# Two 64-byte spacers in on-chip memory: where activations stand modulo 128 bytes, beside the weight rings

## The reference, cut to what matters

```python
x = x + even_mixer(rmsnorm(x, g), w_in, sink, w_out)
x = x + memory_cross_attention(rmsnorm(x, g), rmsnorm(mem, g), wq, wkv, wo)
x = x + conv_mixer(rmsnorm(x, g), w_in, conv_w, conv_b, w_out)
...
a = silu(xb @ w_gate_e[e]) * (xb @ w_up_e[e])
return a @ w_down_e[e]
```

## The kernel before

| tensor | before | modulo 128 | modulo 512 | after | modulo 128 | modulo 512 |
|---|---|---|---|---|---|---|
| `X` | 16512 | 0 | 128 | 16576 | 64 | 192 |
| `xa_hi` | 32896 | 0 | 128 | 32960 | 64 | 192 |
| `xa_lo` | 49280 | 0 | 128 | 49344 | 64 | 192 |
| `cm_hi` | 65664 | 0 | 128 | 65728 | 64 | 192 |
| `cm_lo` | 75904 | 0 | 128 | 75968 | 64 | 192 |
| `U` | 86144 | 0 | 128 | 86208 | 64 | 192 |
| `arena` | 102528 | 0 | 128 | 102592 | 64 | 192 |
| `sq` | 152704 | 0 | 128 | 152768 | 64 | 192 |
| `w_ring`, `ex_rings` | 159040 | 64 | 320 | 159168 | 64 | 448 |
| `hi_ring` | 171328 | 64 | 320 | 171456 | 64 | 448 |
| `lo_ring` | 183616 | 64 | 320 | 183744 | 64 | 448 |
| `yb_lo`, `ex_low` | 195904 | 64 | 320 | 196032 | 64 | 448 |
| `yb_hi`, `ex_raw` | 212288 | 64 | 320 | 212416 | 64 | 448 |

## Time and profile before

### The profile page before, as it was taken

How to read it: one execution, slowest core, us unless ns; L and a number is a source line. 1 busy time by engine, 2 the same in 40 slices (tenths; PEclk the granted TensorE clock), 3 DMA queues, 4 the chain that set the end, 5 groups by cost and what they waited for, 6 DMA issues and landing times.

```text
span 1635.1 us, 20099 instructions
## 1 busy us (share of the span) xinstructions
PE 1594.2 (97%) x7432; PEld 1203.1 (74%) x7432; DVE 844.8 (52%) x1456; ACT 583.8 (36%) x963; POOL 547.7 (33%) x239
## 2 busy tenths in 40 slices
PE   7999989999999999999999999999999999999997
PEld 5888768886888888887877667888877885444543
DVE  5448577125655546354668687343242544443434
ACT  4127544334332225324533342343243333112213
POOL 4441226731444444751334123455424410000000
PEclk9999999999999999999999999999999999999998
DMA  5331224521332323441222113334222349999992
GB/s 187 92 102 39 78 78 124 160 90 60 100 92 91 102 91 98 160 128 40 80 77 69 40 48 94 114 110 136 91 64 91 117 191 356 418 422 421 423 417 82
DMA packets 52787, 235.94 MB, mean 144 GB/s; under 512 B 6240, under 2 KB 7136, under 8 KB 48096
## 3 DMA queue, kind: packets, MB, share of 16 engines
q1 hardware_dynamic: 48960, 222.60, 38.8%
q0 software_dynamic: 2016, 7.34, 1.1%
q10 hardware_dynamic: 1728, 4.87, 0.9%
HBM read 230.59 MB, written 4.19 MB: 144 GB/s over the span
## 4 chain that ended last, share of the span: by engine, by line
PE 90%; DVE 6%; issue 2%; ACT 1%; DMA 0%; SPq 0%; DVEq 0%; ACTq 0%
PE G L1802 69%; PE O L1802 7%; PE S L1802 6%; PE TR L1802 4%; PE TR L1912 2%; DVE sumsq L994 1%; PE G L2374 1%; DVE sq L1054 1%; DMA w_ring<-in_stream_dram 0%; ACT hi_ring L570 0%; DVE U L1025 0%; DVE sumsq L1124 0%; DVE arena L1424 0%; DVE U L1779 0%; DVE arena L1203 0%
## 5 line engine op out<-in xcount | busy, mean ns | idle before, releaser
L535 POOL TENSOR_TENSOR lo_ring<-w_ring,hi_ring 128x1024 fp32r<-128x1024 f32 x219 | 534.0, 2440 | 788.0 <-ACT hi_ring L570 787.7
L570 ACT ACTIVATE hi_ring<-w_ring 128x1024 fp32r<-128x1024 f32 x219 | 231.3, 1059 | 587.4 <-PE G L1802 583.1
L1802 PE MATMUL G<-xa_hi,hi_ring 128*128 128x512 f32 x928 | 378.8, 408 | 9.8 <-DVE xa_lo L1116 9.7
L1802 PE MATMUL G<-xa_hi,lo_ring 128*128 128x512 f32 x928 | 364.9, 393 | 0.0
L1802 PE MATMUL G<-xa_lo,hi_ring 128*128 128x512 f32 x928 | 363.1, 391 | 0.0
L1802 PEld LDWEIGHTS G<-xa_hi,hi_ring 128*128 128x128 f32 x928 | 175.1, 189 | 48.6 <-issue 12.3
L1802 PEld LDWEIGHTS G<-xa_lo,hi_ring 128*128 128x128 f32 x928 | 175.1, 189 | 40.3 <-issue 2.6
L1802 PEld LDWEIGHTS G<-xa_hi,lo_ring 128*128 128x128 f32 x928 | 174.8, 188 | 39.8
L1802 PE MATMUL G<-yb_hi,hi_ring 128*128 128x512 f32 x388 | 154.4, 398 | 3.4 <-ACT arena L668 2.2
L1802 PE MATMUL G<-yb_hi,lo_ring 128*128 128x512 f32 x388 | 151.6, 391 | 0.0
L1802 PE MATMUL G<-yb_lo,hi_ring 128*128 128x512 f32 x388 | 151.4, 390 | 0.0
(11 more groups left out here) (350 smaller groups left out, 2501.4 us busy)
## 6 DMA issues: line engine op xcount, KB each, us to landing
w_ring<-in_stream_dram SPq DMA_DIRECT2D x219, 512.0 KB, 3.5
arena<-in_w_gu_dram SPq DMA_DIRECT2D x16, 2048.0 KB, 11.9
ex_rings<-in_w_dn_dram SPq DMA_DIRECT2D x40, 512.0 KB, 15.8
ex_low<-in_w_gu_dram SPq DMA_DIRECT2D x8, 2048.0 KB, 18.4
ex_rings<-in_w_gu_dram SPq DMA_DIRECT2D x8, 2048.0 KB, 16.0
arena<-in_w_dn_dram SPq DMA_DIRECT2D x16, 512.0 KB, 14.4
sq<-in_w_dn_dram SPq DMA_DIRECT2D x8, 512.0 KB, 18.1
X<-in_x_in_dram SPq DMA_DIRECT2D x8, 256.0 KB, 6.2
```

The costliest lines, as they stand in the source:

```text
L535: nc.gpsimd.tensor_tensor(lo_ring[:, s, :], w_ring[:, s, :], hi_ring[:, s, :], ALU.subtract).then_inc(low, 1)
L570: nc.scalar.activation(hi_ring[:, m % RING, :], w_ring[:, m % RING, :], ACT.Copy).then_inc(high, 1)
L1802: return nc.tensor.matmul(*args, **kw)
```

## The change

Two unused tensors of 16 float32 columns, 64 bytes in a partition, are declared: one ahead of `X`, one ahead of the rings. Everything from `X` to `rcp` moves up by 64 bytes, and the rings, `yb` and the `ex_` buffers by 128. No instruction is added, removed or moved, and each engine's sequence is the same; only the addresses differ.

```diff
+HALF_LINE = 16
...
+        sb("line_a", [P, HALF_LINE])
         X = sb("X", [P, KT, T])
         xa_hi = sb("xa_hi", [P, KT, T], F32R)
...
         rcp = sb("rcp", [P, 4, 2])
+        sb("line_b", [P, HALF_LINE])
         before_experts = ExitStack()
```

## The result

| | before | after |
|---|---|---|
| time, median of 6 runs | 1640.78 us (1638.08 to 1642.35) | 1626.37 us (1622.67 to 1629.88) |
| ratio | | 0.9918, 95% interval 0.9901 to 0.9935 |
| span of the profiled execution | 1635.1 us | 1626.4 us |
| mean granted clock in it | 0.991 | 0.989 |
| forecast | | 1634.1 us, range 1630.0 to 1643.5 |

The account below looks back on a forecast made before the run. PE was taken as the bound: how soon one matmul follows another. Gains of 5.6 + 2.5 + 0.3 + 0.6 less 1.0 lost make 8.0 us, so 1642.1 - 8.0 = 1634.1 us, range 1630 to 1643.5.

Parts of the forecast that it names:

- Equal places bring `yb`'s pace: 512-column fp32r matmuls on PE: equal remainders modulo 128 give 226.7 ns between starts; 8.0 us gained; chance 0.58.
- the five priced terms: Matmul pace on PE: `xa` moving 5.6, rings moving 2.5, `cm` in latents 0.3, scatter 0.6 us gained; 256 columns 1.0 lost.
- The rule behind it, modulo 128: fp32r matmuls: pace set by whether moving and stationary operands have equal remainders modulo 128; 2.2 or 6.6 ns each.
- a period of 256: Operand distances modulo 256 would be 64, 192 and after the change 0; fits all three paces, forecast of 1634.1 us holds.
- The doubt about 512: Slower rival: fp32r pace follows distance modulo 512, the change giving an untried 256; 1647 or 1655 us; chance of slower 0.15.
- `yb` itself, costed at nothing: `yb` moving against rings already has equal remainders and takes 226.7 ns; no term in the sum.
- The 256-column term: Memory tokens: 480 matmuls go from 117.9 to 120.0 ns; 1.0 us lost, bounds 0 and 1.0.
- the waits behind it, costed at nothing: PE behind the memory tokens: no term for waits; ACT, DVE and POOL groups expected as before.
- "The change doesn't touch" what lies between span and median: Whole kernel: median of runs lies 7.0 us above the profiled span, kept unchanged, so 1642.1 us was the starting point.
- the rivals: fp32r pace: only part is the remainder, 1639 or 1637.2 us (0.13); nothing changes, 1642 (0.14); slower, 1647 or 1655 (0.15).
- The page of the Trainium skill that would make the sum 0: PE operand reads: separate port for weight loads, only crossing 16-byte lines costs, so moving by 64 bytes gains 0.
- The expert stage, plain float32, DVE over `X` and `yb`, and DMAs, costed at nothing: Quads about 32.2 us, float32 matmuls 606 ns, DVE passes 683 and 689 ns, DMA at 421 GB/s; no term.

Follow-up runs that it names:

- d = 128: Kernel before plus only a 192-byte spacer ahead of the rings; `xa` start minus ring start is 128 modulo 256; 1640.73 beside 1640.26 us, ratio 1.0009.
- the first experiment: Kernel before plus two spacers of 128 bytes each, ahead of `X` and ahead of the rings; 1645.92 us, ratio 1.0038.
- the slow placements: Kernel before plus both spacers of 128 bytes (1645.92 us), or only one ahead of the rings: 192 (1640.73), 160 (1645.58), 32 bytes (1647.38).

## Why the prediction was right, and where it failed

- *Equal places bring `yb`'s pace.* Right in the traces: 226.7 ns for all 512-column pairs, -8.5 us where -8.0 was forecast. Each of the five priced terms came within 0.2 us.
- *The rule behind it, modulo 128.* It was the change's, and the prediction took it while noting that a period of 256 fits as well. The kernel with equal remainders modulo 128 and d = 128 runs at 232.3 ns: what counts is the distance modulo 256, and the change hits its one fast place because both conditions hold in it. As a test of the words "modulo 128" that was luck: a spacer of 192 bytes obeys them too and gains nothing. The doubt about 512 is settled by the spacer of 320 bytes.
- *`yb` itself, costed at nothing.* Missed, 0.7 us. Where `yb` tiles follow `xa` tiles one by one, they had up to ten slow starts each time behind the change of operand, 24 times; with equal distances the slow starts are gone.
- *The 256-column term, "1.0 us lost", and the waits behind it, costed at nothing.* This is the step that failed. The size in nanoseconds is right. But I took it for a loss on PE alone and left every wait as it was ("ACT, DVE and POOL groups as before"). The 50 ns for each unit of memory keys take away POOL's lead over DVE's addition, and two waits of 1.55 us go. So the slower part of the change brings 3.1 us where the forecast has a loss of 1.0, and some 1.3 to 2.4 us more at low clock (estimated above). The order of DVE and POOL alone, without the placement, makes the kernel 4.1 us faster. The signs stood in the trace of before: `DVE sumsq L994 1%` in the chain, and two starts 60 ns apart behind it, one of them of 2.87 us instead of 0.68.
- *"The change doesn't touch" what lies between span and median.* Wrong: executions differ in their granted clock (in the 18 runs beside the first experiment 1636.8 us goes with 0.992 and 1644.1 us with 0.987), and the change takes away waits that drops follow.
- *The range.* Its low end came from the bounds of the pace terms alone (they reach 1634.1 - 2.1 = 1632.0 us, where the prediction writes 1631.5) and a little on top. No mechanism on the faster side stood among the rivals; the one of another sign was looked for on the slower side only.
- *The page of the Trainium skill that would make the sum 0, "SBUF — State Buffer".* The runs decide against it for fp32r matmuls: places that are all multiples of 32 bytes, thus of 16, differ by 3% (226.7 to 234.3 ns).
- *The expert stage, plain float32, DVE over `X` and `yb`, and DMAs, costed at nothing.* Right: 32.22 us a quad, 607 and 685 ns. The earlier trace rows were misread on the way: `arena` is in neither of them; `U` stands in both, and `ex_low` or `U` itself moves.

What stays open: why only one difference of eight is fast, whether it is the moving operand's reads meeting those of the next weight load (no run separates them), why some differences have two paces, and the 2 to 3 us of the slow placements.

## What to carry to other kernels

With fp32r matmuls of 512 columns in long runs, lay the moving and the stationary operand at a multiple of 256 bytes from each other; one spacer of 64 bytes did it here, worth 1 to 3% of the pace by the placement that it replaces. With 256 columns that placement was among the slowest. A small change of pace is priced twice: by its length, and by what it does to orders that are decided by some tens of nanoseconds. So look, for each wait in the chain, whether the engine waited for was itself stretched by a neighbour that started just ahead. And a single profiled execution is no average: compare its clock and its span with the other runs' before building on the distance.

## What the hardware showed that I had not expected

- fp32r, 512 columns: 226.7 ns at difference 0 modulo 256, 232.4 to 234.3 at 96, 128, 160 and others, two paces at 64 (228.9 and 233.3) with the same addresses. With 256 columns the order is nearly the other way: 120.0 ns at 0, 113.4 or 117.8 at 192.
- DVE's addition of 128x512: 0.68 us when it starts 40 ns ahead of POOL's pass or, by the record, up to 20 ns behind; 2.87 us when it starts 60 ns behind. One ACT instruction in each layer, which delays POOL, makes the kernel 4.1 us faster.
- Behind a stall of PE of 1.67 us the granted clock fell to 0.50, which is 1.2 GHz, for 3.4 us in the profiled executions of some kernels, and not in that of the kernel before, which has the same stall.
